# Expert weights by pairs: one 4 MB load for the gate or up matrices of two experts, products on the two halves of the rows

## What is computed

```python
g_idx = jnp.argmax(g_logits, axis=-1)                 # one of 8 groups
top_val, top_idx = lax.top_k(e_logits, TOP_K)         # two of its 8 experts
expert_id = g_idx[:, None] * EXPERTS_PER_GROUP + top_idx
...
def run_block(args):
    xb, e = args
    h = jax.nn.silu(xb @ w_gate[e]) * (xb @ w_up[e])
    return h @ w_down[e]
...
y = jnp.zeros((N, D), x.dtype).at[slot_tok].add(ys * slot_gate[:, None])
```

## Time and profile before

| | |
|---|---|
| median of 3 runs | 1483.08 us (1483.07 to 1483.86) |
| the profiled execution | 1482.48 us |
| its span, first to last instruction | 1480.7 us |
| mean granted PE clock | 0.946 |
| PE busy | 1235.6 us (83%) |
| DVE, ACT, POOL busy | 496.0, 293.6, 53.2 us |
| moved by DMA | 493.01 MB, mean 333 GB/s |

### The profile page before, as it was taken

The page is one execution under the profiler, slowest core; times in us unless marked ns, Lnnn a source line. Parts: engine busy times, 40 slices in busy tenths (PEclk is TensorE's granted clock), DMA queues, the critical chain, the costliest instruction groups (busy, mean ns, idle before and its releaser), DMA issues.

```text
span 1480.7 us, 34399 instructions
## 1 busy us (share of the span) xinstructions
PE 1235.6 (83%) x15164; PEld 947.1 (64%) x15164; DVE 496.0 (33%) x1038; ACT 293.6 (20%) x740; POOL 53.2 (4%) x89
## 2 busy tenths in 40 slices
PE   9999977677767777686777786877799999999998
PEld 6566756556556556565555565655678687888854
DVE  1663222122121120221221202212278555566644
ACT  3433221012021120210111202101232222211100
POOL 4101000000000000000000000000010110000000
PEclk9999999899899997998999989989999999999999
DMA  9539999999999999999999999999993351555420
GB/s 343 193 140 380 381 428 428 428 428 428 428 429 428 429 428 429 428 429 428 429 428 428 428 428 429 428 428 428 408 336 114 128 184 59 171 171 170 171 85 29
DMA packets 79759, 493.01 MB, mean 333 GB/s; under 512 B 4924, under 2 KB 28696, under 8 KB 55144
## 3 DMA queue, kind: packets, MB, share of 16 engines
q1 hardware_dynamic: 77792, 486.69, 80.1%
q0 software_dynamic: 1520, 4.91, 1.1%
q10 hardware_dynamic: 408, 0.86, 0.2%
HBM read 491.39 MB, written 1.05 MB: 333 GB/s over the span
## 4 chain that ended last, share of the span: by engine, by line
DMA 53%; PE 44%; DVE 1%; issue 1%; ACT 0%; POOL 0%; SPq 0%; DVEq 0%; POOLq 0%
DMA ring<-in_w_gate_dram 46%; PE bank L1678 8%; PE bank L1230 6%; DMA ring<-in_w_down_dram 5%; PE bank L881 4%; PE bank L1725 4%; PE bank L1358 4%; PE bank L1043 2%; DMA ring<-in_w_up_dram 2%; PE bank L1544 1%; PE bank L805 1%; PE bank L1654 1%; PE bank L1407 1%; PE bank L781 1%; PE bank L1587 1%; PE bank L1624 1%
## 5 line engine op out<-in xcount | busy, mean ns | idle before, releaser
L1230 PE MATMUL bank<-ring,big 128*32 128x128 f32 x8192 | 302.6, 309 | 176.0 <-DMA ring<-in_w_gate_dram 117.6
L1230 PEld LDWEIGHTS bank<-ring,big 128*32 128x32 f32 x8192 | 261.3, 125 | 226.8 <-DMA ring<-in_w_gate_dram 89.0
L2592 DVE TENSOR_TENSOR big<-big,bank 128x128 f32<-128x128 f32 x64 | 24.1, 376 | 498.5 <-PE bank L1230 498.5
L1259 PE MATMUL bank<-ring,big 128*32 128x256 f32 x1536 | 101.0, 406 | 33.6 <-DMA ring<-in_w_down_dram 33.1
L1982 ACT ACTIVATE big<-bank 32x256 f32<-32x256 f32 x96 | 35.9, 374 | 388.9 <-PE bank L1259 387.7
L2604 DVE COPY big<-bank 32x256 f32<-32x256 f32 x96 | 40.5, 422 | 195.7 <-PE bank L1259 194.2
L1259 PEld LDWEIGHTS bank<-ring,big 128*32 128x32 f32 x1536 | 50.3, 114 | 65.0 <-issue 28.3
L1245 PEld LDWEIGHTS bank<-aux,c 128*128 128x128 f32 x512 | 65.5, 200 | 15.0 <-issue 15.0
L1245 PE MATMUL bank<-aux,c 128*128 x512 | 74.3, 290 | 0.0
L881 PE MATMUL bank<-ring,xT 128*128 128x512 f32 (+1 forms) x160 | 67.9, 563 | 0.2 <-DVE xT L2231 0.2
L1205 PE MATMUL bank<-big,xn 128*128 128x128 f32 x512 | 65.1, 288 | 0.0
(11 more groups left out here) (482 smaller groups left out, 1691.3 us busy)
## 6 DMA issues: line engine op xcount, KB each, us to landing
ring<-in_w_up_dram SPq DMA_DIRECT2D x64, 2048.0 KB, 26.8
ring<-in_w_gate_dram SPq DMA_DIRECT2D x63, 2048.0 KB, 26.0
ring<-in_w_down_dram SPq DMA_DIRECT2D x62, 2048.0 KB, 27.1
ring<-in_w_gate_up_dram SPq DMA_DIRECT2D x22, 1024.0 KB, 7.7
ring<-in_w_down_dram SPq DMA_DIRECT2D x14, 1024.0 KB, 6.9
ring<-in_w_in_dram SPq DMA_DIRECT2D x12, 1024.0 KB, 14.8
ring<-in_w_in_dram SPq DMA_DIRECT2D x3, 2048.0 KB, 25.1
ring<-in_w_out_dram SPq DMA_DIRECT2D x2, 2048.0 KB, 18.5
```

The source lines that it names most:

```text
L1230: i = pe.matmul(dst[TOK * j:TOK * (j + 1), 0:P], xg[:, k, TOK * q:TOK * (q + 1)], w[:, k, j * P:(j + 1) * P], start=(k == 0), stop=(k == K ...
L1259: i = pe.matmul(bank[6 + q % 2][TOK * m:TOK * (m + 1), 0:SEQ], hT[:, q % 2, TOK * k:TOK * (k + 1)], w[:, k, SEQ * m:SEQ * (m + 1)], start= ...
```

## The change

The order of loads becomes gate 0, gate 1, up 0, up 1, down 0, down 1, then the same for experts 2 and 3. The gate matrices of two experts are brought by one load of 4 MB into two neighbouring slots: the first expert on partitions 0 to 63, the second on 64 to 127, 16 of the 1024 features to a partition, 32 KB in one piece. The same holds for the up matrices. Down matrices are loaded as before. The first four loads ahead of the loop, which get their slots one at a time, bring a half of each row (`first_half_load`), and the first reload of a pair comes as 1, 1 and 2 MB.

`xg` has the features in 16 steps of 64 partitions, expert 0 (or 2) on the lower half, expert 1 (or 3) on the upper. The gather writes 64 columns at a time into the two halves. `hidden` does a pair: 16 steps, in each four column tiles of 32, and for each the two experts on rows 0 to 63 and 64 to 127, with results in two banks. One product with the identity stands ahead of each pair and one in the middle of the first. PE's order goes by pairs, and ACT and DVE follow it. The gain is loaded twice, once for each half.

```diff
-MOE_UNITS = [(part, q) for q in range(BATCH) for part in ("gate", "up", "down")]
+MOE_UNITS = [(part, 2 * h + r) for h in range(BATCH // 2) for part in ("gate", "up", "down") for r in range(2)]
+HALF = P // 2
+KH = 16
...
-        moe_gain = sb("moe_gain", KD)[:, :]
+        moe_gain = sb("moe_gain", KH)[:, :]
...
+        def two_slots(u):
+            g = (PRE_UNITS + u) % RING
+            return ring[:, g * SLOT:(g + 2) * SLOT]
...
-        xg = cut(KD * P).rearrange("p (k s) -> p k s", k=KD)
+        xg = cut(KH * HALF).rearrange("p (k s) -> p k s", k=KH)
...
+            def pair_rows(part, experts):
+                return t_in["w_" + part][0, experts].rearrange("e (p k) c -> (e p) (k c)", p=HALF)
+            def loads(us):
+                return [u for u in us if MOE_UNITS[u][0] == "down" or MOE_UNITS[u][1] % 2 == 0]
             def moe_load(u, expert):
                 part, _ = MOE_UNITS[u]
-                w = t_in["w_" + part][0, expert].rearrange("e (p k) c -> p (e k c)", p=P)
-                sp.dma_start(slot(PRE_UNITS + u), w).then_inc(S(f"moe_in{u % RING}"), 16)
+                if part == "down":
+                    sp.dma_start(slot(PRE_UNITS + u), t_in["w_down"][0, expert].rearrange("e (p k) c -> p (e k c)", p=P)
+                                 ).then_inc(S(f"moe_in{u % RING}"), 16)
+                else:
+                    sp.dma_start(two_slots(u), pair_rows(part, expert)).then_inc(S(f"moe_in{u % RING}"), 16)
+            def first_half_load(u):
+                part, q = MOE_UNITS[u]
+                k0 = q % 2 * SLOT
+                sp.dma_start(slot(PRE_UNITS + u), pair_rows(part, bass.ds(0, 2))[:, k0:k0 + SLOT]
+                             ).then_inc(S(f"moe_in{u - 1 if q % 2 else u + 1}"), 16)
...
                 part, q = MOE_UNITS[u - RING]
+                if part != "down":
+                    q += 1
                 n = done + q + 1 if u >= RING else done - BATCH + q + 1
                 sp.wait_ge(*at({"gate": "moe_g", "up": "moe_gu", "down": "moe_d"}[part], n))
             def experts_of(b, u):
-                return bass.ds(b * BATCH + MOE_UNITS[u][1], 1)
+                return bass.ds(b * BATCH + MOE_UNITS[u][1], 1 if MOE_UNITS[u][0] == "down" else 2)
...
-            part, q = MOE_UNITS[RING]
-            w = t_in["w_" + part][0, bass.ds(q, 1)].rearrange("e (p k) c -> p (e k c)", p=P)
-            dst, h = slot(PRE_UNITS + RING), SLOT // 2
+            w, dst = pair_rows(MOE_UNITS[RING][0], bass.ds(MOE_UNITS[RING][1], 2)), two_slots(RING)
             for n in range(2):
                 sp.wait_ge(*at("moe_g0", n + 1))
-                sp.dma_start(dst[:, n * h // 2:(n + 1) * h // 2], w[:, n * h // 2:(n + 1) * h // 2]).then_inc(S("moe_next"), 16)
-            sp.wait_ge(*at("moe_g", 1))
-            sp.dma_start(dst[:, h:], w[:, h:]).then_inc(S(f"moe_in{RING % RING}"), 16)
+                sp.dma_start(dst[:, n * SLOT // 2:(n + 1) * SLOT // 2], w[:, n * SLOT // 2:(n + 1) * SLOT // 2]
+                             ).then_inc(S("moe_next"), 16)
+            sp.wait_ge(*at("moe_g", 2))
+            sp.dma_start(dst[:, SLOT:], w[:, SLOT:]).then_inc(S(f"moe_in{RING % RING}"), 16)
             with sp.Fori(0, NB - 1) as b:
-                for u in range(RING + 1, 2 * RING):
+                for u in loads(range(RING + 2, 2 * RING)):
                     moe_slot_free(u, b * BATCH)
                     moe_load(u, experts_of(b, u))
-                for u in range(RING + 1):
+                for u in loads(range(RING + 1)):
...
-                    sp.wait_ge(S("moe_d" if part == "down" else "moe_gu"), rounds * NE + (q + 2 - BATCH))
+                    sp.wait_ge(S("moe_d" if part == "down" else "moe_gu"), rounds * NE + ((q if part == "down" else q | 1) + 2 - BATCH))
...
-            load(moe_gain, t_in["norm2_gain"][0].rearrange("(p k) -> p k", p=P), "moegain_in")
+            for r in range(2):
+                load(moe_gain[HALF * r:HALF * r + HALF, :], t_in["norm2_gain"][0].rearrange("(p k) -> p k", p=HALF), "moegain_in")
...
+            def pair_slots(t, r):
+                return sel[:, t, :].rearrange("p (h r j) -> p r h j", h=2, r=2)[:, r]
...
             def gather(it, half):
                 pe.wait_ge(*at("moe_sel", it + 1))
-                for k in range(4 * half, 4 * half + 4):
+                for k in range(8 * half, 8 * half + 8):
                     for t in range(TT):
-                        i = pe.matmul(bank[2 + half][:, (k % 4) * P:(k % 4 + 1) * P], xn[:, t, k * P:(k + 1) * P],
-                                      sel[:, t, :], start=(t == 0), stop=(t == TT - 1))
+                        for r in range(2):
+                            i = pe.matmul(bank[2 + half][HALF * r:HALF * r + HALF, (k % 8) * HALF:(k % 8 + 1) * HALF],
+                                          xn[:, t, k * HALF:(k + 1) * HALF], pair_slots(t, r), start=(t == 0), stop=(t == TT - 1))
...
-                def hidden(part, q, dst, signal):
-                    arrive(part, q)
-                    if MOE_UNITS[RING] == (part, q):
+                def hidden(part, h, dst, signal):
+                    arrive(part, 2 * h)
+                    if h == 0:
+                        pe.wait_ge(*at("moe_in1" if part == "gate" else "moe_in3", 16))
+                    elif part == "gate":
                         pe.wait_ge(*at("moe_next", 32))
-                    w = slot(PRE_UNITS + MOE_UNITS.index((part, q))).rearrange("p (k c) -> p k c", k=KD)
-                    for k in range(KD):
-                        if (part, q) == ("gate", 0) and k in (2, 4):
+                    w = two_slots(MOE_UNITS.index((part, 2 * h))).rearrange("p (k c) -> p k c", k=KH)
+                    pe.matmul(dst[0][:, 0:P], ident, ident, start=True, stop=True)
+                    for k in range(KH):
+                        if (part, h) == ("gate", 0) and k in (4, 8):
                             i.then_inc(S("moe_g0"), 1)
-                        if (part, q, k) == ("gate", 0, 4):
+                        if (part, h, k) == ("gate", 0, 8):
                             pe.wait_ge(*at("moe_xg_v", it + 1))
+                            pe.matmul(bank[6][:, 0:P], ident, ident, start=True, stop=True)
                         for j in range(4):
-                            i = pe.matmul(dst[TOK * j:TOK * (j + 1), 0:P], xg[:, k, TOK * q:TOK * (q + 1)],
-                                          w[:, k, j * P:(j + 1) * P], start=(k == 0), stop=(k == KD - 1),
-                                          tile_position=(0, TOK * j))
-                    i.then_inc(S(signal), 1)
+                            for r in range(2):
+                                o = HALF * r
+                                i = pe.matmul(dst[r][TOK * j:TOK * (j + 1), 0:P], xg[o:o + HALF, k, TOK * h:TOK * (h + 1)],
+                                              w[o:o + HALF, k, j * P:(j + 1) * P], start=(k == 0), stop=(k == KH - 1),
+                                              tile_position=(o, TOK * j))
+                                if (k, j) == (KH - 1, 3):
+                                    i.then_inc(S(signal), 1)
...
-                for q in range(BATCH):
-                    if q < 2:
-                        pe.wait_ge(*at("moe_xadd", it * 4 + 1 + 2 * q))
-                    hidden("gate", q, bank[q % 2], "moe_g")
-                    if q == 0:
-                        pe.wait_ge(*at("moe_selg", it + 1))
-                        for t in range(TT):
-                            i = pe.transpose(bank[5][:, t * P:(t + 1) * P], sel_gate[:, t, :], ident)
-                        i.then_inc(S("moe_selT_tp"), 1)
-                        pe.wait_ge(*at("moe_selT", it + 1))
-                    if q == 2:
-                        memory_rows(2)
-                    if q == 3:
-                        pe.wait_ge(*at("moe_xadd", it * 4 + 4))
-                        gather(it + 1, 0)
-                        gather(it + 1, 1)
-                    hidden("up", q, bank[5], "moe_gu")
-                    if q < 2:
-                        memory_rows(q)
-                    if q == 2:
-                        memory_rows(3)
-                    if q < BATCH - 1:
-                        down(q)
+                pe.wait_ge(*at("moe_xadd", it * 4 + 3))
+                hidden("gate", 0, (bank[0], bank[1]), "moe_g")
+                pe.wait_ge(*at("moe_selg", it + 1))
+                for t in range(TT):
+                    i = pe.transpose(bank[5][:, t * P:(t + 1) * P], sel_gate[:, t, :], ident)
+                i.then_inc(S("moe_selT_tp"), 1)
+                pe.wait_ge(*at("moe_selT", it + 1))
+                hidden("up", 0, (bank[5], bank[7]), "moe_gu")
+                memory_rows(0)
+                memory_rows(1)
+                down(0)
+                down(1)
+                memory_rows(2)
+                memory_rows(3)
+                pe.wait_ge(*at("moe_xadd", it * 4 + 4))
+                gather(it + 1, 0)
```

(61 more changed lines are left out.)

54 lines of the change are left out of this document (17 added, 37 removed).

## The result

The changed kernel took 1804.72 us (median of 6 runs, 1793.27 to 1807.48) against 1483.07: a ratio of 1.2151, interval 1.213 to 1.2173. The profiled execution took 1797.94 us. The forecast was 1487.0 with a range to 1503: wrong, 321.7 us more than before where 3.9 were forecast.

A forecast was written before the change was run, and what follows sets the result against it. The prediction took weight loads over DMA to bound the expert stage (150 to 1066 us). Its terms, -4.6 loads, +0.3 start, +0.2 tail and +8 code, summed to +3.9 us: 1487.0 us, range 1478 to 1503.

The forecast's parts named there:

- The code: PE's loop body grows to 2,793 records and is refetched each pass: 8 us lost, bounds 0 and 100.
- PE's 43 us per batch stay near 44; its cover is the 15.7 us: Expert stage: PE's work per batch hardly grows and stays covered by the batch's 58.7 us of loads.
- The last sign that the prediction gave for being wrong: Expert stage: the prediction is wrong if PE has no wait left for the gate loads.
- Rival 2: Loop fetching costs more, packets hitting some engines twice as often or PE stalling on each: 1492 to 1504 us; chance 11%.
- Against it: the steady first pass: Argument against costlier fetching: 160 to 188 us shows 427 GB/s against 428 later, although code packets came in the first pass.
- The loads: Gate and up loads become 61 of 4 MB with 32 KB rows: 4.6 us gained, bounds 0 and 7.
- The products: Gate and up pairs: 128 half-row products take 3.7 us if eight tiles run together, 7.4 if four; 3.7 taken.
- rival 3: Row halves of the products don't run side by side: +10 to +50 us, 1493 to 1533; chance 9%.
- Coarser slots: SP's load slots come free only when both experts of a pair are done; the load queue hides it: cost nothing.
- The start: First reload near 150 us is released 0.45 us later, as a bigger piece: +0.3 us, bounds -1 and +4.
- The tail: After the last up pair lands, PE's remaining work nearly fits before the last byte: +0.2 us, bounds 0 and 1.5.
- Rival 1: PE's loop is kept or refetched for free: 1479.0 us, between 1476 and 1482; chance 28%.

The follow-up runs named there:

- 36 added: Kernel before the change plus 36 tiny one-column products per batch behind the memory rows, body 1,747 instructions: 1509.0 us, ratio 1.0177.
- both kernels with 32 KB rows whose code stays: Changed kernel with 6 of 16 steps per gate and up pair, 1480.6 us; and with all half-row products in a quarter of the instructions, 1483.3 us.
- 4 MB loads with rows of 16 KB: Changed kernel's 4 MB loads and pair order, but products on all 128 rows as before, body 1,603 instructions: 1484.1 us, ratio 1.0002.
- the short code: Changed kernel with 512-column half-row products, a quarter of the instructions, partial sums added afterwards: 1487.4 us; with first gate pair ahead and slots freed sooner, 1483.3 us.
- the first run: First timing of the kernel before with 36 tiny products per batch: 1591.6 us, not used because the granted clock was 0.85 outside the loop.
- 11 steps: Changed kernel with 11 of the 16 steps of each gate and up pair, 5 left out of the computation: 1588.7 us.
- 160 tiny products: Kernel before the change plus 160 tiny one-column products per batch behind the memory rows, body 2,243 instructions: 1664.7 us.

## Why the prediction was wrong

**The failed step is "The code", in its price.** That the loop would not stay was forecast, though no row showed it, and the packets too (about 190; 228 came, 13 per pass instead of 11). But the step priced a fetch by its bytes on the DMA engines alone, 6.3 us spread evenly, 8 taken, 100 as the far end. What it assumed of a fetch holds. The trace of before has 31,229 records of PE, its sequencer's among them; less 15 repeated passes of 1,603 these are 7,184, and 28 packets of 16.4 KB for them are 257 to a packet, 64 bytes each. The loop of 1,603 stays: in its repeated passes one packet came. That packets don't fall evenly fits the sixteen arrivals of a load, 13.7 us apart with 36 added instead of 2.7. But no run shows the 8 us: while the loads were the bound, 8.4 packets a pass cost 1.5 to 1.7 us per batch and 26 us in all, and the changed kernel lost 321.7. The step left out that PE stands still. It also left "PE's 43 us per batch stay near 44; its cover is the 15.7 us" as if code came free: measured per batch, 54.5 busy, 21.6 waiting for issue and 1.7 for DVE and ACT, 77.9 in all where the cover ended at 58.7. The last sign that the prediction gave for being wrong came true: PE has no wait left for the gate loads. Rival 2 named "PE stalls on each" and then priced packets only, 1492 to 1504; even the engines' part by itself, 13 packets at 1.6 / 8.4 us, would be an estimated 2.5 us per pass, 37 in all.

"Against it: the steady first pass" read the wrong row. The DMA rate of 160 to 188 us shows no fetch because the loads were the bound: a stall of PE under 15.7 us of cover leaves no trace in it. And the first pass of before is not that of after. With 257 instructions to a packet, 128 records and their weight loads are about one packet; they lasted 3.68 us and now last 2.03. Seven packets came from 146 to 191 us before, twelve from 146 to 222 us after. PE's waits for issue in the first pass, after (146 to 222 us) and before (146 to 191 us):

```profile
PE bank L1273 <- issue: 15.2, 7, 3.9
```

```profile
PE bank L1259 <- issue: 0.5, 1, 0.5
```

The 15.2 us are half of the 31.4 us by which that batch ends late. That before stood for only 0.5 us because its instructions lasted longer is an estimate; no run changed that alone.

What PE itself does at a fetch, the rows above show: it stands for 5.3 to 5.9 us at the head of a pass and for 239.1 us in all at L1273, and the edge lies between 1,667 and 1,747 instructions.

**The loads: right.** 0.30 us per batch were forecast from the line through two row lengths; 58.7 became 58.3 and 428 became 431 GB/s in both kernels with 32 KB rows whose code stays, while 4 MB loads with rows of 16 KB gave 58.6 and 428. **The products: right.** Eight tiles run at once, 16 ns a record at a clock of 1.00; rival 3 is out. The gather takes 19.8 / 5 = 4.0 us, 4.4 forecast. **Coarser slots: right**, nothing (1.0002). **The start: mis-sized.** Taken at +0.3 with bounds -1 and +4, it is 5 us, of which 2.4 to 2.7 are waits for issue. **The tail** can't be read in the changed kernel, where PE bounds there as well. Rival 1 is what the short code gave back: about 1479 was forecast for a kept loop, 1483.3 came; the difference is about that of the start.

## What to carry to other kernels

Count PE's instructions in a loop before doubling its products: here a body of 1,667 stayed and one of 1,747 was fetched anew in 14 or 15 of 15 repeated passes. The DMA rate hardly announced it while loads were the bound (421 GB/s with 36 added, 428 before); the packets of the instruction queue did (154 instead of 28). Price a fetch twice, as bytes on the engines and as PE standing still, and compare PE's busy time plus its waits for issue with the cover, batch by batch. Where smaller tiles are wanted, make each product longer so that the count stays small: with 512 columns to a product the body had 1,433 instructions, and 28 packets came.

## What the runs showed of the hardware

- PE's loop of 1,667 instructions is not fetched again (28 packets in the whole run), one of 1,747 is: 154 packets, nine in each of fourteen of the fifteen repeated passes, and 163, nine in each of fifteen, in the first run. A fetched pass brings more than its body fills: nine packets where 1,747 instructions fill 6.8 at 257 to a packet, 13 where 2,839 fill 11.0.
- At the head of each of the fifteen fetched passes of the changed kernel PE stands for 5.3 to 5.9 us. It stands again inside the pass: 21.6 us per batch in all after, with 16 ns records at a clock of 1.00, and (31.7 + 21.9 + 11.0 + 11.0 + 0.6) / 5 = 15.2 us with 11 steps at 2,199. A body of 2,243 with 160 tiny products, where PE is busier, waits (26.3 + 6.8) / 5 = 6.6 us.
- PE's waits for issue of over 1 us in the changed kernel end 1.2 to 2.5 us after an instruction packet has come (111 waits behind 200 us).
- With 8.4 instruction packets per pass on average a batch is 1.5 to 1.7 us longer at a DMA share of 1.00, near three times the packets' even share of 0.6, and the sixteen arrivals of a load take 13.7 us instead of 2.7 (median, 36 added).
- The granted clock was 0.50 right behind 5.26 us of standing still, and 0.74 to 0.85 over single batches of the changed kernel (0.80 over five) instead of 0.91. PE's busy time grew by 11 us per batch. Some 2.3 us of this are the identity products (11.7 / 5 at L1263); most of the rest is the same work at the lower clock: the half-row products took 18.3 us in short code and 111.9 / 5 = 22.4 after, down (L1303) 44.0 / 5 = 8.8 us where 28.0 / 5 = 5.6 had done in short code. No run held the stalls and changed the clock, so their shares are not separated further.
